# Each step of four attentions in two halves between the blocks of the weight groups

## The chip, the cores and the metric

One Trainium2 chip, of which the kernel uses one core. The core has a tensor engine (PE; its weight loads are listed apart as PEld), a vector engine (DVE), a scalar engine (ACT), GpSimd (POOL) and SyncE (SP), which issues the transfers. Each engine works through its own instructions strictly in order, and they wait for each other by semaphores. The metric is the device time of one execution in microseconds.

## The reference

Two transformer blocks in float32 on one sequence of 512 tokens and 1024 features.

```python
def first_block(x, ...):
    h = rms_norm(x, norm1_g)
    qa, ka, va, hy_in, qc, kc, vc, gate_logits = split(h @ w_in)
    out_a = window_attention(rope(norm(qa)), rope(norm(ka)), va, sink_a)      # 8 heads, |t - s| <= 128
    out_b = hyena_branch(hy_in, ...)
    out_c = rms_norm(diff_attention(rope(norm(qc)), rope(norm(kc)), vc, lam)) # 4 heads, softmax1 - lam * softmax2
    merged = g[0] * (out_a @ w_oa) + g[1] * (out_b @ w_ob) + g[2] * (out_c @ w_oc)
    x = x + merged @ w_out
    return x + (silu(h2 @ w1) * (h2 @ w3)) @ w2                               # h2 = rms_norm(x, norm2_g)

def second_block(x, ...):
    fq, fk, fv, f_logit, sq, sk, sv = split(rmsnorm(x) @ w_in_2)
    o_fox = fox_attention(fq, fk, fv, log_sigmoid(f_logit + bias))            # 8 heads, causal, softmax with decay
    # stick breaking, 8 heads: z = q.k / 8, s < t
    # A[t, s] = sigmoid(z[t, s]) * prod over s < j < t of (1 - sigmoid(z[t, j]));  o_sb = A @ v
    x = x + concat(rmsnorm(o_fox), rmsnorm(o_sb)) @ w_out_2
    u = causal_dwconv(rmsnorm(x) @ w_up)
    return rmsnorm(x + (silu(gate) * val) @ w_down)
```

## The kernel before, in words

**Weights and blocks.** All projections are streamed: 240 slots of 128 x 1024 numbers come from HBM, and each is split into a high and a low part of a reduced type, `whi` on ACT (L1357) and `wlo` on DVE (L785; on POOL, L1797, for `qc`, `kc`, `vc` and the hyena groups), so that three matmuls give the accuracy of one in float32. A group of weights (`qc`, `kc`, `gA0`, `sv`, `fq`, ...) is 4 or 2 slots, and a slot is worked off in four blocks, each of 6 matmuls over 512 columns into banks `ps0` to `ps3` of the accumulator memory. After the last slot of a group each block's bank is evacuated by ACT or DVE.

**Work beside.** The four attentions have no stretch of their own, apart from the end of the last one. Each is a Python generator, one copy for each engine, put in `flow.beside`. After each block `slots` calls `flow.pump` for some steps of it: `group(..., rate)` says how many steps go into the four blocks of a slot, so rate 2 puts one step after every second block, rate 4 one after every block. What a step has on an engine stands in that engine's queue at that place. `window` (36 steps, rate 2) runs beside `qc`, `kc`, `vc`, `gA0`, `gA1`; `differential` (22 steps, rate 2) beside `bA0`, `bA1`, `gC0`, `gC1`; `stick` (37 steps) beside `sv` (rate 1), `fq` (2), `fk` and `fv` (4); `fox` (38 steps) starts in `fv` with three steps, and the rest follows with no blocks between ("the drain"). Rotary work of `qc` and `kc` (DVE L952 to L970, partly POOL) stands in `flow.later` between the slots.

**A step.** Unit u is one head of one block of 128 query tokens. PE has three kinds of work in step u: `turn`, the transposes (L353) of an earlier unit's weights; `scores` of unit u (or u and u + 1 at every other step) into `ps4`/`ps5`; `values` of a unit still earlier. In the window attention DVE's `lowest(u)` reads the scores and takes a row extreme (L1003), ACT's `shares(u)` takes the exponential (L1491, L1493), DVE's `shares(u-1)` divides (L1009 to L1013), and ACT copies the transposed tile `PT` (L1500). In the differential attention DVE has `highest(u)` (two of L1057, L1059) and `combine(u-1)` (L1066 to L1072, which makes `Pc`); after the fourth head of a block of queries its output goes through squares (DVE L1087), a root and a scale on POOL (L1919 to L1925, which write `ocs`), four transposes of `ocs` into `ps6` in PE's step (L353), and `ochi`/`oclo` (ACT L1546, DVE L1091).

**The stick-breaking step.** For unit u, with n the width of its scores (units 0 to 7 have 512 columns, 8 to 15 have 128, 16 to 23 have 384, 24 to 31 have 256): ACT `copy(u)` brings the scores from `ps4`/`ps5` to `zb` (L1646); DVE `parts(u)` makes |z| and min(-z, 0) from it (L1191, L1192); ACT `logs(u)` (L1651, L1653); DVE `sums(u)`, a scan (L1199); POOL adds, `sum(u)` (L1964); ACT `weights(u)` (L1658); PE `turn(u)`; DVE `evac(u)` to `PT` (L1207); PE `values(u)`. In step u DVE has `sums(u-2)`, `evac(u-4)`, `parts(u)` in this order, and POOL `sum(u-2)`. ACT has `copy(u)`, `logs(u-1)`, `weights(u-2)`. The copy waits for the scores alone, and for POOL's sum three units back, which frees its `zb`.

**Fox step.** In the drain PE has `scores(u)`, `turn(u-3)`, `values(u-5)`, DVE `lowest(u)` and the evacuation of even units, ACT `shares(u)` and that of odd units.

Of the kernel before, what the change touches and what calls it, by code (L numbers as in the profile page):

```python
# [129 lines left out]
def build(nc, d, out):  # L130
# [208 lines left out]
    def tensor_program(t):  # L339
# [165 lines left out]
        def window():  # L505
# [107 lines left out]
        def stick():  # L613
# [49 lines left out]
        def fox():  # L663
# [68 lines left out]
        rotary_group("qc", 2, 4, 2)  # L732
        rotary_group("kc", 3, 4, 2)
        group("vc", hT, h_ready(0), lambda b: (vc_c, b + 1), 2)
        flow.flush()
        for half in range(2):
            group("gA%d" % half, hT, h_ready(0), lambda b: (g_t, 8 + 4 * half + b + 1), 2)
        flow.drain()
        flow.beside.append(differential())
        for half in range(2):  # L740
            group("bA%d" % half, lambda k: (oahi[:, k, :], oalo[:, k, :]), lambda k, b: w.wait_ge(oa_lo, 4),
                  lambda b: (b_v, 8 + 4 * half + b + 1), 2)
        for half in range(2):
            group("gC%d" % half, hT, h_ready(0), lambda b: (g_t, 16 + 4 * half + b + 1), 2)
# [15 lines left out]
        group("sv", hT, h_ready(2), lambda b: (sv_c, b + 1))  # L760
        flow.beside.append(fox())
        group("fq", hT, h_ready(2), lambda b: (h_v, 2 * (b // 2) + 2) if b % 2 else (h_a, 2 * (b // 2) + 2), 2)
        group("fk", hT, h_ready(2), lambda b: (h_v, 4 + 2 * (b // 2) + 2) if b % 2 else (h_a, 4 + 2 * (b // 2) + 2), 4)
        group("fv", hT, h_ready(2), lambda b: (fv_c, b + 1), 4)
# [10 lines left out]
    def vector_program(v):  # L775
# [215 lines left out]
        def window():  # L991
# [57 lines left out]
        def differential():  # L1049
# [129 lines left out]
        def stick():  # L1179
# [42 lines left out]
        def fox():  # L1222
# [33 lines left out]
            for u in range(38):  # L1256
                while u == 3 and not fox_go:
                    yield
                if u < 32:
                    lowest(u)  # L1260
                if 3 <= u < 35 and (u - 3) % 2 == 0:
                    evac(u - 3)
# [39 lines left out]
        group("qc", rotary(2, 8), 2)  # L1302
        group("kc", rotary(3, 8), 2)
        group("vc", none, 2)
        flow.flush()
        for half in range(2):
            group("gA%d" % half, none, 2)
        flow.drain()
        flow.beside.append(differential())
        for half in range(2):  # L1310
            group("bA%d" % half, branch(1, half), 2)
        for half in range(2):
            group("gC%d" % half, none, 2)
# [12 lines left out]
        group("sv", none)  # L1326
        flow.beside.append(fox())
        group("fq", heads_out(Qf), 2)
        group("fk", heads_out(Kf), 4)
        group("fv", none, 4)  # L1330
# [15 lines left out]
    def scalar_program(a):  # L1346
# [138 lines left out]
        def window():  # L1485
# [21 lines left out]
            for u in range(36):  # L1507
                if 3 <= u < 35:
                    evac(u - 3)
                if u < 32:  # L1510
# [10 lines left out]
        def differential():  # L1521
# [27 lines left out]
            for u in range(22):  # L1549
                if 2 <= u < 18:  # L1550
                    evac(u - 2)
                if u < 16:
# [87 lines left out]
        def stick():  # L1640
# [19 lines left out]
            for u in range(37):  # L1660
                if u < 32:
                    copy(u)
                if 1 <= u <= 32:
                    logs(u - 1)
                if 2 <= u < 34:
                    weights(u - 2)
                if u in (15, 23, 31):
# [14 lines left out]
        def fox():  # L1682
# [14 lines left out]
            for u in range(38):  # L1697
                while u == 3 and not fox_go:
                    yield
                if u < 32:  # L1700
                    shares(u)
                if 3 <= u < 35 and (u - 3) % 2:
                    evac(u - 3)
# [46 lines left out]
        group("qc", rotary(2, 8, qcT), 2)  # L1750
        group("kc", rotary(3, 8, kcT), 2)
        group("vc", values, 2)
        flow.flush()
        for half in range(2):
            group("gA%d" % half, gates(1, half), 2)
        flow.drain()
        flow.beside.append(differential())
        for half in range(2):
            group("bA%d" % half, none, 2)
        for half in range(2):  # L1760
            group("gC%d" % half, gates(2, half), 2)
# [484 lines left out]
```

## Time and profile before

| | |
|---|---|
| median of 3 runs | 1731.5 us (1728.58 to 1731.97) |
| the profiled execution | 1728.6 us, of which its span is 1726.8 us |
| PE busy | 1648.0 us (95%), granted clock 0.989 of full on average |
| DVE, ACT, POOL busy | 833.2, 658.0, 271.0 us |

| stretch | us | PE idle in it, us |
|---|---|---|
| window, 311 to 480 | 169 | 4.9 |
| differential, 487 to 598 | 111 | 8.2 |
| stick beside `sv` and `fq`, 1105 to 1170 | 65 | 4.1 |
| stick beside `fq` end, `fk`, `fv`, 1170 to 1250 | 80 | 9.6 |
| fox, the drain, 1250 to 1306 | 56 | 0.8 |

The times in the rows below count from the start of the span. A row of the order in time gives its start, its duration, the engine, the line, what it writes and reads (without the numbers of the buffers), how many instructions it stands for, and in square brackets how long the engine had been idle and what ended that.

### The profile page before, as it was taken

How to read it: one execution, taken by the hardware profiler on the slowest of the kernel's cores; microseconds unless marked ns; L12 is line 12 of the kernel's file. 1: busy time of each engine (PE TensorE's matmuls, PEld its weight loads, DVE VectorE, ACT ScalarE, POOL GpSimd, SP SyncE). 2: the span in 40 equal slices, each digit the busy share in tenths (PEclk: the TensorE clock that was granted, in tenths of full speed). 3: DMA queues.
4: the chain of work that ended last, by engine and by line, in shares of the span. 5: the costliest groups of instructions: out<-in, count | busy, mean ns of one | idle time of the engine just before them, and what ended most of it. 6: DMA issues, size and time to landing. Idle time of an engine off the chain costs nothing.

```text
span 1726.8 us, 19076 instructions
## 1 busy us (share of the span) xinstructions
PE 1648.0 (95%) x7552; PEld 1301.6 (75%) x7552; DVE 833.2 (48%) x1332; ACT 658.0 (38%) x1150; POOL 271.0 (16%) x280
## 2 busy tenths in 40 slices
PE   5999998999999999999999998898999999999997
PEld 3566787767766787888888886676678788888886
DVE  5446455366356464333332224376663465556323
ACT  4332223454444433333222223366563344444221
POOL 3443205462012111000000002023200100000001
PEclk9999999999999999999999999999999999999999
DMA  6111112211121332333332321221102233233332
GB/s 227 56 67 47 49 49 85 80 50 62 61 62 49 110 98 73 98 98 98 98 98 98 97 87 63 93 69 42 50 13 74 74 97 98 95 94 92 111 98 72
DMA packets 39221, 139.51 MB, mean 81 GB/s; under 512 B 4331, under 2 KB 4971, under 8 KB 38940
## 3 DMA queue, kind: packets, MB, share of 16 engines
q1 hardware_dynamic: 39132, 138.29, 25.0%
q8 instruction: 60, 0.98, 0.2%
q14 instruction: 29, 0.24, 0.0%
HBM read 136.14 MB, written 2.10 MB: 80 GB/s over the span
## 4 chain that ended last, share of the span: by engine, by line
PE 84%; DVE 7%; POOL 4%; ACT 3%; issue 2%; DMA 1%; SPq 0%; DVEq 0%; POOLq 0%; ACTq 0%
PE ps L350 80%; PE ps L353 3%; DVE raw L970 1%; ACT whi L1357 1%; POOL small L1817 1%; POOL st L1881 1%; POOL small L1811 0%; DVE wlo L785 0%; ACT junk L1369 0%; DMA x<-in_x 0%; POOL small L1814 0%; DVE st L1057 0%; DVE xs L796 0%; DVE W L1199 0%; DVE olo L1162 0%
## 5 line engine op out<-in xcount | busy, mean ns | idle before, releaser
L785 DVE TENSOR_TENSOR wlo<-wraw,whi 128x1024 fp32r<-128x1024 f32 (+2 forms) x220 | 267.0, 1214 | 527.3 <-ACT whi L1357 527.1
L350 PE MATMUL ps<-hThi,whi 128*128 128x512 f32 x1128 | 453.6, 402 | 2.2 <-DVE hTlo L801 1.4
L1357 ACT ACTIVATE whi<-wraw 128x1024 fp32r<-128x1024 f32 (+2 forms) x244 | 253.0, 1038 | 511.6 <-PE ps L350 506.0
L350 PE MATMUL ps<-hThi,wlo 128*128 128x512 f32 x1128 | 441.0, 391 | 0.0
L350 PE MATMUL ps<-hTlo,whi 128*128 128x512 f32 x1128 | 440.9, 391 | 0.0
L350 PEld LDWEIGHTS ps<-hThi,whi 128*128 128x128 f32 x1128 | 212.7, 189 | 57.4 <-issue 15.7
L350 PEld LDWEIGHTS ps<-hThi,wlo 128*128 128x128 f32 x1128 | 212.6, 189 | 45.4
L350 PEld LDWEIGHTS ps<-hTlo,whi 128*128 128x128 f32 x1128 | 212.8, 189 | 44.5 <-issue 2.9
L350 PE MATMUL ps<-whi,achi 128*128 128x512 f32 x352 | 136.9, 389 | 0.0
L350 PE MATMUL ps<-wlo,achi 128*128 128x512 f32 x352 | 136.9, 389 | 0.0
L350 PE MATMUL ps<-whi,aclo 128*128 128x512 f32 x352 | 136.9, 389 | 0.0
L350 PE MATMUL ps<-whi,hThi 128*128 128x512 f32 (+1 forms) x288 | 115.2, 400 | 0.0
L1811 POOL TENSOR_SCALAR small<-small 128x1 f32<-128x1 f32 x20 | 10.0, 499 | 649.7 <-ACT junk L1369 648.5
L350 PE MATMUL ps<-wlo,hThi 128*128 128x512 f32 (+1 forms) x288 | 110.6, 384 | 0.0
L350 PE MATMUL ps<-whi,hTlo 128*128 128x512 f32 (+1 forms) x288 | 110.5, 384 | 0.0
L350 PEld LDWEIGHTS ps<-wlo,achi 128*128 128x128 f32 x352 | 66.1, 188 | 13.8
L350 PEld LDWEIGHTS ps<-whi,achi 128*128 128x128 f32 x352 | 66.1, 188 | 13.7
L350 PEld LDWEIGHTS ps<-whi,aclo 128*128 128x128 f32 x352 | 66.1, 188 | 13.7
L1797 POOL TENSOR_TENSOR wlo<-wraw,whi 128x1024 fp32r<-128x1024 f32 x24 | 58.8, 2453 | 82.4 <-ACT whi L1357 82.4
L350 PEld LDWEIGHTS ps<-whi,hThi 128*128 128x128 f32 x288 | 55.6, 193 | 13.6 <-issue 4.4
L350 PEld LDWEIGHTS ps<-whi,hTlo 128*128 128x128 f32 x288 | 55.4, 192 | 10.7
L350 PEld LDWEIGHTS ps<-wlo,hThi 128*128 128x128 f32 x288 | 55.6, 193 | 9.5 <-issue 0.5
(272 smaller groups left out, 2151.0 us busy)
## 6 DMA issues: line engine op xcount, KB each, us to landing
wraw<-in_ws SPq DMA_DIRECT2D x236, 512.0 KB, 3.5
x<-in_x SPq DMA_DIRECT2D x4, 512.0 KB, 7.8
x<-in_x SPq DMA_DIRECT2D x1, 2048.0 KB, 8.4
out<-xs SPq DMA_DIRECT2D x8, 256.0 KB, 2.0
dec<-in_dec SPq DMA_DIRECT2D x1, 1024.0 KB, 15.9
wraw<-in_ws SPq DMA_DIRECT2D x4, 256.0 KB, 2.6
vec<-in_vec SPq DMA_DIRECT2D x1, 788.0 KB, 4.9
w<-in_w SPq DMA_DIRECT2D x1, 512.0 KB, 14.3
```

The lines of the kernel that those rows point to most:

```text
L350: return t.matmul(o, l, r, start=first, stop=last)
L353: return t.transpose(ps[b][:, c * 128:(c + 1) * 128], src, ident)
L785: v.tensor_tensor(wlo[h][:, 0:width(i)], wraw[h][:, 0:width(i)], whi[h][:, 0:width(i)].bitcast(F32), ALU.subtract).then_inc(lo_done[h], 1)
L970: v.tensor_tensor(r_, q0, q1, ALU.add).then_inc(r_a, 1)
L1357: a.activation(whi[h][:, 0:width(i)], wraw[h][:, 0:width(i)], ACT.Copy).then_inc(hi_done[h], 1)
L1797: g.tensor_tensor(wlo[h][:, 0:width(i)], wraw[h][:, 0:width(i)], whi[h][:, 0:width(i)].bitcast(F32), ALU.subtract).then_inc(lo_done[h], 1)
L1811: g.tensor_scalar(small[:, i:i + 1], small[:, c:c + 1], 1.0 / D, EPS, ALU.mult, ALU.add).then_inc(n_rs, 1)
L1817: g.tensor_tensor(small[:, 8 + i:9 + i], small[:, 4 + i:5 + i], col("mhalf"), ALU.pow).then_inc(n_rs, 1)
L1881: g.tensor_tensor(ss, ms, col("mhalf", 0, n_heads), ALU.pow).then_inc(r_r, 1)
```

## The change

The generators of all four attentions yield twice in each step, and the rates are doubled, so that a step covers the same blocks as before. Where a step has two blocks (`window`, `differential`, and `stick` beside `fq`) its first half stands after the first of them and its second half after the second, which was the place of the whole step; `stick` beside `sv` has a step in four blocks, its halves after the second and the fourth. Where a step has one block (`stick` beside `fk` and `fv`) or none (the drain of `fox`) the two halves follow each other directly. The first half holds `turn` on PE, and on the others what belongs to earlier units; the second holds `scores` and `values`, and what belongs to unit u. For that the order inside a step changes at these places: DVE's `shares(u-1)` and `combine(u-1)` now stand ahead of `lowest(u)` and `highest(u)`, ACT's `logs(u-1)` and `weights(u-2)` ahead of `copy(u)`, and in `fox` the transposes and evacuations ahead of `scores`, `lowest` and `shares`. No instruction is added or taken away on any engine.

```diff
@@ PE: window, differential, stick
             for u in range(36):
                 if 3 <= u < 35:
                     turn(u - 3)
+                yield
                 if u < 32 and u % 2 == 0:
                     scores(u)
                     scores(u + 1)
...
             for u in range(22):
                 if 2 <= u < 18:
                     turn(u - 2)
+                yield
                 if u < 16:
                     scores(u)
...
             for u in range(37):
                 if 4 <= u < 36:
                     turn(u - 4)
+                yield
                 if u < 32 and u % 2 == 0:
                     scores(u)
@@ PE: fox
+                if 3 <= u < 35:
+                    turn(u - 3)
+                yield
                 if u < 32:
                     scores(u)
-                if 3 <= u < 35:
-                    turn(u - 3)
@@ the rates, the same on every engine
-        rotary_group("qc", 2, 4, 2)
+        rotary_group("qc", 2, 4, 4)
...
-        group("sv", hT, h_ready(2), lambda b: (sv_c, b + 1))
+        group("sv", hT, h_ready(2), lambda b: (sv_c, b + 1), rate=2)
...
-        group("fv", hT, h_ready(2), lambda b: (fv_c, b + 1), 4)
+        group("fv", hT, h_ready(2), lambda b: (fv_c, b + 1), 8)
@@ DVE: window
             for u in range(36):
+                if 1 <= u <= 32:
+                    shares(u - 1)
+                yield
                 if u < 32:
                     lowest(u)
-                if 1 <= u <= 32:
-                    shares(u - 1)
@@ DVE: differential
             for u in range(22):
+                if 1 <= u <= 16:
+                    combine(u - 1)
+                yield
                 if u < 16:
                     highest(u)
-                if 1 <= u <= 16:
-                    combine(u - 1)
@@ DVE: stick
                 if 4 <= u < 36:
                     evac(u - 4)
+                yield
                 if u < 32:
                     parts(u)
@@ ACT: stick
             for u in range(37):
-                if u < 32:
-                    copy(u)
                 if 1 <= u <= 32:
                     logs(u - 1)
                 if 2 <= u < 34:
                     weights(u - 2)
+                yield
+                if u < 32:
+                    copy(u)
```

ACT beside `fk`, before: two steps of the stick-breaking attention, from the copy of one unit's scores on (`zb` are the copied scores, `Lb` the logarithms and weights of units one and two back).

```order
L1646 ACTIVATE zb0_188<-ps4 128x384
L1651 ACTIVATE Lb2_185<-Lb2_185 128x384
L1653 ACTIVATE Lb2_185<-Lb2_185,vec_60 128x384
L1658 ACTIVATE Lb1_184<-Lb1_184 128x384
L1646 ACTIVATE zb1_189<-ps5 128x384
L1651 ACTIVATE Lb3_186<-Lb3_186 128x384
L1653 ACTIVATE Lb3_186<-Lb3_186,vec_60 128x384
```

The same instructions now (the lines are ten further down):

```order
L1661 ACTIVATE Lb2_185<-Lb2_185 128x384
L1663 ACTIVATE Lb2_185<-Lb2_185,vec_60 128x384
L1668 ACTIVATE Lb1_184<-Lb1_184 128x384
L1656 ACTIVATE zb0_188<-ps4 128x384
L1661 ACTIVATE Lb3_186<-Lb3_186 128x384
L1663 ACTIVATE Lb3_186<-Lb3_186,vec_60 128x384
L1668 ACTIVATE Lb2_185<-Lb2_185 128x384
```

The copy of unit u moved from ahead of the logarithms to behind the weights of unit u - 2.

DVE in the differential attention, before: the unit that ends the second block of queries (its two row extremes), the combination of the unit before it, the squares of that block's output, and then the split of a weight slot.

```order
L1057 TENSOR_REDUCE st_129<-ps5 128x1
L1059 TENSOR_SCALAR st_129<-st_129 128x1
L1066 RECIPROCAL st_129<-st_129 128x1
L1068 SCALAR_TENSOR_TENSOR st_129<-st_129,small_61 128x1
L1070 RECIPROCAL st_129<-st_129 128x1
L1072 SCALAR_TENSOR_TENSOR Pc0_136<-Pc1_137,st_129,Pc0_136 128x512
L1087 TENSOR_REDUCE st_129<-oc_142 128x4
L785 TENSOR_TENSOR wlo1_58<-wraw1_52,whi1_55 128x1024
```

The same place now:

```order
L1039 SCALAR_TENSOR_TENSOR gate1_108<-gate1_108,ps2 128x512
L1071 RECIPROCAL st_129<-st_129 128x1
L1073 SCALAR_TENSOR_TENSOR st_129<-st_129,small_61 128x1
L1075 RECIPROCAL st_129<-st_129 128x1
L1077 SCALAR_TENSOR_TENSOR Pc0_136<-Pc1_137,st_129,Pc0_136 128x512
L1039 SCALAR_TENSOR_TENSOR gate1_108<-gate1_108,ps3 128x512
L1062 TENSOR_REDUCE st_129<-ps4 128x1
L1064 TENSOR_SCALAR st_129<-st_129 128x1
L1062 TENSOR_REDUCE st_129<-ps5 128x1
L1064 TENSOR_SCALAR st_129<-st_129 128x1
L1092 TENSOR_REDUCE st_129<-oc_142 128x4
L789 TENSOR_TENSOR wlo1_58<-wraw1_52,whi1_55 128x1024
```

The combination moved ahead of the extremes, and ahead of the evacuation of the second of two blocks; the squares follow the extremes directly.

PE in the window attention, beside `qc`, at the first transposes of a unit:

```order
 L350 MATMUL ps2<-whi0_54,hTlo_50 128x512
+L353 MATMUL ps6<-vec_60,T8_0_121 128x128 x2
 L350 MATMUL ps3<-whi0_54,hThi_49 128x512
 L350 MATMUL ps3<-wlo0_57,hThi_49 128x512
...
 L350 MATMUL ps3<-wlo0_57,hThi_49 128x512
 L350 MATMUL ps3<-whi0_54,hTlo_50 128x512
-L353 MATMUL ps6<-vec_60,T8_0_121 128x128 x2
```

The transposes moved ahead of one block; scores and values stand where they stood.

## Rows read from the trace of the kernel before

**Rows 1.** Table by stretch: start:end, us, busy of PE, PEld, DVE, ACT, POOL, clock, DMA, GB/s.

```profile
1170.00:1250.00 80.00, 70.45 (x385) 52.81 (x383) 54.86 (x112) 50.09 (x120) 23.84 (x34) 0.98 0.14 47
```

**Rows 2.** PE's waits by what it waited for: us in total, times, longest us.

```profile
PE ps L353 <- POOL ocs L1925: 7.0, 3, 3.0
...
PE ps L353 <- DVE PT L1207: 4.8, 7, 1.7
```

**Rows 3.** Order in time on PE, window attention, around two transposes of a unit.

```profile
325.88 0.38 PE L353 MATMUL ps<-vec,T 128*128 128x128 f32 x2
326.01 0.48 PE L350 MATMUL ps<-whi,hThi 128*128 128x512 f32 x1
...
328.85 0.38 PE L353 MATMUL ps<-vec,T 128*128 128x128 f32 x2
329.16 0.70 PE L350 MATMUL ps<-kaT,qaT 64*128 64x256 f32 x4
```

**Rows 4.** Order in time, window attention, rotary work on DVE just before 356.45.

```profile
356.45 0.60 DVE L1003 CUSTOM_DVE_ANT_0 T<-ps,maskA,small 128x384 f32<-128x384 f32 x1
...
357.10 0.61 ACT L1491 ACTIVATE T<-T,st 128x384 f32<-128x384 f32 x1 [5.62 <-DVE st L1003]
...
357.12 0.91 PE L350 MATMUL ps<-kaT,qaT 64*128 64x384 f32 x2 [1.48 <-DVE st L1003]
...
357.93 0.60 DVE L1003 CUSTOM_DVE_ANT_0 T<-ps,maskA,small 128x384 f32<-128x384 f32 x1
```

**Rows 5.** Order in time, differential attention: the first wait, and the outputs' way.

```profile
501.64 0.66 PE L353 MATMUL ps<-vec,Pc 128*128 128x128 f32 x4 [1.27 <-DVE Pc L1072]
...
533.51 0.75 DVE L1091 SCALAR_TENSOR_TENSOR oclo<-ps,vec,ochi 128x512 fp32r<-128x512 f32 x1 [0.52 <-ACT ochi L1546]
...
548.63 0.69 DVE L1057 TENSOR_REDUCE st<-ps 128x1 f32<-128x512 f32 x1 [1.89 <-PE ps L350]
...
550.21 0.16 DVE L1066 RECIPROCAL st<-st 128x1 f32<-128x1 f32 x1
...
551.40 0.68 DVE L1087 TENSOR_REDUCE st<-oc 128x4 f32<-128x512 f32 x1
...
554.82 1.04 POOL L1925 TENSOR_TENSOR ocs<-ocs,st 128x512 f32<-128x512 f32 x1
...
555.91 0.66 PE L353 MATMUL ps<-vec,ocs 128*128 128x128 f32 x4 [1.96 <-POOL ocs L1925]
```

**Rows 6.** Order in time, stick-breaking attention, two units of 384 columns.

```profile
1203.86 0.49 ACT L1646 ACTIVATE zb<-ps 128x384 f32<-128x384 f32 x1 [2.79 <-PE ps L350]
...
1204.38 0.56 DVE L1191 SCALAR_TENSOR_TENSOR Lb<-zb 128x384 f32<-128x384 f32 x1 [1.18 <-ACT zb L1646]
...
1205.52 0.96 DVE L1199 TENSOR_TENSOR_SCAN W<-W,Lb 128x384 f32<-128x384 f32 x1 [0.31 <-ACT Lb L1653]
...
1206.55 1.00 POOL L1964 TENSOR_TENSOR Lb<-zb,W 128x384 f32<-128x384 f32 x1 [3.37 <-DVE W L1199]
...
1206.88 1.09 DVE L1191 SCALAR_TENSOR_TENSOR Lb<-zb 128x384 f32<-128x384 f32 x1
...
1207.58 0.53 ACT L1658 ACTIVATE Lb<-Lb 128x384 f32<-128x384 f32 x1 [0.32 <-POOL Lb L1964]
...
1210.21 1.22 DVE L785 TENSOR_TENSOR wlo<-wraw,whi 128x1024 fp32r<-128x1024 f32 x1
```

**Rows 7.** The same attention: the copies of units 17 and 31, and between them.

```profile
1185.13 0.47 ACT L1646 ACTIVATE zb<-ps 128x384 f32<-128x384 f32 x1
...
1214.11 0.68 DVE L1278 COPY Kf<-ps 64x512 f32<-64x512 f32 x1 [0.23 <-PE ps L350]
...
1218.62 0.73 POOL L1964 TENSOR_TENSOR Lb<-zb,W 128x256 f32<-128x256 f32 x1 [1.16 <-DVE W L1199]
...
1233.33 0.36 ACT L1646 ACTIVATE zb<-ps 128x256 f32<-128x256 f32 x1
```

**Rows 8.** The table by stretch, 3.5 us in the stick-breaking attention after a wait of PE.

```profile
1199.00:1202.50 3.50, 3.50 (x13) 2.54 (x12) 2.49 (x4) 2.04 (x6) 3.16 (x5) 0.56 0.00 0
```

More of the change, by code:

```diff
@@ L731, in tensor_program @@
         flow.beside.append(window())
-        rotary_group("qc", 2, 4, 2)
-        rotary_group("kc", 3, 4, 2)
-        group("vc", hT, h_ready(0), lambda b: (vc_c, b + 1), 2)
+        rotary_group("qc", 2, 4, 4)
+        rotary_group("kc", 3, 4, 4)
+        group("vc", hT, h_ready(0), lambda b: (vc_c, b + 1), 4)
         flow.flush()
         for half in range(2):
-            group("gA%d" % half, hT, h_ready(0), lambda b: (g_t, 8 + 4 * half + b + 1), 2)
+            group("gA%d" % half, hT, h_ready(0), lambda b: (g_t, 8 + 4 * half + b + 1), 4)
         flow.drain()
@@ L741, in tensor_program @@
             group("bA%d" % half, lambda k: (oahi[:, k, :], oalo[:, k, :]), lambda k, b: w.wait_ge(oa_lo, 4),
-                  lambda b: (b_v, 8 + 4 * half + b + 1), 2)
+                  lambda b: (b_v, 8 + 4 * half + b + 1), 4)
         for half in range(2):
-            group("gC%d" % half, hT, h_ready(0), lambda b: (g_t, 16 + 4 * half + b + 1), 2)
+            group("gC%d" % half, hT, h_ready(0), lambda b: (g_t, 16 + 4 * half + b + 1), 4)
         flow.drain()
@@ L1258, in fox @@
                     yield
+                if 3 <= u < 35 and (u - 3) % 2 == 0:
+                    evac(u - 3)
+                yield
                 if u < 32:
                     lowest(u)
-                if 3 <= u < 35 and (u - 3) % 2 == 0:
-                    evac(u - 3)
                 if u == 8:
@@ L1301, in vector_program @@
         flow.beside.append(window())
-        group("qc", rotary(2, 8), 2)
-        group("kc", rotary(3, 8), 2)
-        group("vc", none, 2)
+        group("qc", rotary(2, 8), 4)
+        group("kc", rotary(3, 8), 4)
+        group("vc", none, 4)
         flow.flush()
         for half in range(2):
-            group("gA%d" % half, none, 2)
+            group("gA%d" % half, none, 4)
         flow.drain()
@@ L1310, in vector_program @@
         for half in range(2):
-            group("bA%d" % half, branch(1, half), 2)
+            group("bA%d" % half, branch(1, half), 4)
         for half in range(2):
-            group("gC%d" % half, none, 2)
+            group("gC%d" % half, none, 4)
         flow.drain()
@@ L1699, in fox @@
                     yield
+                if 3 <= u < 35 and (u - 3) % 2:
+                    evac(u - 3)
+                yield
                 if u < 32:
                     shares(u)
-                if 3 <= u < 35 and (u - 3) % 2:
-                    evac(u - 3)
                 if u == 7:
@@ L1749, in scalar_program @@
         flow.beside.append(window())
-        group("qc", rotary(2, 8, qcT), 2)
-        group("kc", rotary(3, 8, kcT), 2)
-        group("vc", values, 2)
+        group("qc", rotary(2, 8, qcT), 4)
+        group("kc", rotary(3, 8, kcT), 4)
+        group("vc", values, 4)
         flow.flush()
         for half in range(2):
-            group("gA%d" % half, gates(1, half), 2)
+            group("gA%d" % half, gates(1, half), 4)
         flow.drain()
@@ L1758, in scalar_program @@
         for half in range(2):
-            group("bA%d" % half, none, 2)
+            group("bA%d" % half, none, 4)
         for half in range(2):
-            group("gC%d" % half, gates(2, half), 2)
+            group("gC%d" % half, gates(2, half), 4)
         flow.drain()
@@ L1774, in scalar_program @@
         flow.beside.append(stick())
-        group("sv", copied(sv, sv_c))
+        group("sv", copied(sv, sv_c), rate=2)
         flow.beside.append(fox())
-        group("fq", heads_out(Qf), 2)
-        group("fk", heads_out(Kf), 4)
-        group("fv", copied(fv, fv_c), 4)
+        group("fq", heads_out(Qf), 4)
+        group("fk", heads_out(Kf), 8)
+        group("fv", copied(fv, fv_c), 8)
         fox_go.append(True)
@@ L2001, in gpsimd_program @@
             group("bB%d" % half, none, 2)
-        flow.beside.append(iter(range(36)))
-        group("qc", rotary(2, 8), 2)
-        group("kc", rotary(3, 8), 2)
-        group("vc", none, 2)
+        flow.beside.append(iter(range(72)))
+        group("qc", rotary(2, 8), 4)
+        group("kc", rotary(3, 8), 4)
+        group("vc", none, 4)
         flow.flush()
         for half in range(2):
-            group("gA%d" % half, none, 2)
+            group("gA%d" % half, none, 4)
         flow.drain()
@@ L2011, in gpsimd_program @@
         for half in range(2):
-            group("bA%d" % half, branch(1, half), 2)
+            group("bA%d" % half, branch(1, half), 4)
         for half in range(2):
-            group("gC%d" % half, none, 2)
+            group("gC%d" % half, none, 4)
         flow.drain()
@@ L2026, in gpsimd_program @@
         flow.beside.append(stick())
-        group("sv", none)
+        group("sv", none, rate=2)
         flow.beside.append(fox())
-        group("fq", none, 2)
-        group("fk", none, 4)
-        group("fv", none, 4)
+        group("fq", none, 4)
+        group("fk", none, 8)
+        group("fv", none, 8)
         fox_go.append(True)
```

18 lines of the change are left out of this document (12 added, 6 removed).

## The prediction, made before the kernel ran

> **What bounds the kernel now.** I read the table of times first, then the table by stretch, then PE's list of waits, and last the order in time at the places that this list names. PE is busy for 1648.0 of 1726.8 us, so work that the others do costs nothing unless PE waits for it, and the four attentions are to be judged by PE's idle time: 4.9, 8.2, 4.1, 9.6 and 0.8 us in the five stretches of the second table. The largest is the stick-breaking attention beside the end of `fq`, `fk` and `fv`, with PE busy for 70.45 of 80 us and no other engine over 54.86 [rows 1]: there PE waits for a chain of engines and not for a full one. The list of waits gives 7.0 us to POOL's `ocs`, in the differential attention, and 4.8 us to the evacuation `PT` in the stick-breaking one [rows 2].
>
> **The change on PE.** The instructions are the same; what is new is that a block stands between transposes and scores. In the window attention two transposes cost 0.13 us if a block follows and 0.31 us if scores follow [rows 3]. But the block that was one run of 12 matmuls becomes two of 6, and starting again costs something: the block at 326.01 begins with 0.48 us in place of 0.39. From these I take 0.14 us for the restart and 0.09 us for scores that follow a block (the same 0.09), so 0.13 + 0.14 + 0.09 - 0.31 = +0.05 us in a step with scores, and nothing in one with values alone; a mean of 0.03 us. That is 32 steps x 0.03 = +1.0 in the window attention, 16 x 0.03 = +0.5 in the differential one and 8 x 0.03 = +0.2 in the stick-breaking one beside `fq`. Beside `fk` and `fv` and in the drain no block stands between the halves, so PE's order in the former is as it was. The bounds are 0 and 3 us in all.
>
> **Window attention.** Elsewhere than at the rotary work DVE has time to spare and its new order costs nothing. At the rotary work it is behind, and there it now does `shares(u-1)` ahead of `lowest(u)`. [Rows 4] show one such place: `lowest` at 356.45 lets PE's scores start at 357.12, after a wait of 1.48 us; `lowest` of the next unit comes at 357.93, so the shares between them take 1.48 - 0.60 = 0.88 us. In the new order these 0.88 us stand ahead of the first `lowest`, and PE waits so much longer; and the next shares have to wait for ACT's exponential (0.61 us and two short ones, about 1.2 us), which the old order covered with the next `lowest`. I count two such places at 0.88 us less a little that transposes win by earlier shares: **+1.5 us**, bounds -1 and +6 (five places at 1.2 us).
>
> **Differential attention.** The first wait, 1.27 us for `Pc` at 501.64 [rows 5], should go, since `combine` no longer stands behind `highest`: -1.3. For the output of a block of queries the way is `highest`, `combine`, squares, four instructions on POOL, transposes. At 550.21 to 551.40 `combine` takes 1.19 us of it, PE waits 1.96 us at the end of it, and DVE has been idle for 1.89 us before `highest` [rows 5], so here the combination finds room and PE's wait shrinks by up to 1.19. What is late next is `ps6`: it is free only after `oclo`, which waits for ACT's `ochi` (row at 533.51), which stands behind an exponential of the unit then under way; the following unit's transposes now come one block sooner. I allow 0.3 us for that: -0.9. For the first output DVE has no such idle time (in its order two gate evacuations stand there back to back, and the combination moves between them): -0.2. The third has the list's longest wait of 3.0 [rows 2] and room: -1.1. Sum -1.3 - 0.9 - 0.2 - 1.1 = **-3.5 us**, bounds -5 and -0.5.
>
> **Stick-breaking attention.** Before, ACT copied unit u's scores as soon as they were there. Now `copy(u)` stands behind `weights(u-2)`. These wait for POOL's `sum(u-2)`, which waits for DVE's `sums(u-2)`, which stands in DVE's queue right behind `parts(u-1)`, which wait for `copy(u-1)`. So there is a closed loop of one step, where before two steps shared one. Its length for 384 columns from [rows 6]: copy to `parts` 1204.38 - 1203.86 = 0.52; `parts` to scan 1205.52 - 1204.38 less the 0.31 that the scan waited for ACT = 0.83; scan to POOL 1.03; POOL to weights 1.03; weights to the next copy 0.43 (0.53 less the 0.1 by which such rows overlap). Sum 3.84 us. For 256 columns POOL's row is 0.73 against 1.00 [rows 7]; at about that ratio the loop is 2.8 us. From the copy of unit 17 to that of unit 31 are 7 steps of 384 columns, one between and 6 of 256: 7 x 3.84 + 3.3 + 6 x 2.8 = 47.0. Into DVE's place between `parts` and `sums` fall further the splits of three slots (1.22 each, [rows 6]) and two pairs of `Kf` copies (2 x 0.68 each, [rows 7]): 47.0 + 3.7 + 2.7 = 53.4 us. The trace of before has 1233.33 - 1185.13 = 48.2 us [rows 7]. That is +5.2 us. After it PE had little slack, so I let it through: **+5.2 us**. Bounds: 0, if `wlo` and `Kf` find DVE idle and PE's waits of before are the same waits; +10, if output tiles and `whi` on ACT fall in the loop too. With 512 columns, beside `sv`, the loop is about 4.7 us by the same scaling and a step has a slot's time there: nothing. With 128 columns it is shorter than a step's blocks: nothing.
>
> **Drain of fox.** PE is idle for 0.8 of 56 us. The new order puts transposes ahead of scores; the transposes' input is three units old and ready: 0, bounds -0.3 and +1.
>
> **Sum.** +1.7 (PE) + 1.5 - 3.5 + 5.2 = +4.9 us. On the profiled execution, 1728.6 us, that gives 1733.5; this execution is 2.9 us below the median of the three, 1731.5, so against the median it is **1736.4**, which I round to 1736.5.
>
> **The rivals.** *The loop is hidden.* If three quarters of the loop's interruptions fall into DVE's idle time and PE's slack takes the rest, stick costs 0 to 1 us, and the sum is +1.7 + 1.5 - 3.5 + 0.5 = +0.2: 1731.7. For it speaks that before, too, the splits stood in the chain and PE kept 3.4 us a step; against it, that 3.84 us is more than 3.4 without any interruption. *Faster.* DVE's `parts` take 0.56 us at 1204.38 and 1.09 us at 1206.88, beside a POOL instruction that began at 1206.55 [rows 6]. In the new order `parts(u)` come after POOL's sum by their place in the loop and are never beside it. If this is what made `PT` late, the 4.8 us of [rows 2] go, the loop costs nothing, and with both attentions of the first block as above: +1.7 + 1.5 - 3.5 - 4.8 = -5.1: 1726.4. The Trainium skill, "Advanced Engine Details and Errata", section "GPSIMD Details", says that GpSimd shares a read and a write interface with the vector engine and conflicts with its instructions that have two SBUF inputs. `parts` begin with such an instruction, so by that rule the trace agrees, and this rival is the time that it gives. Against it: shorter `parts` shorten the loop, but I have already counted them at 0.56. *Worse.* From five rotary places at 1.2 us, +6 in place of +1.5, and PE waiting longer at each step of the stick-breaking loop, so that its clock falls: in 3.5 us after a wait it was at 0.56 [rows 8], which is 1.5 us of work lost each time. It decides if PE's waits in the loop pass what they were at 1196. With three falls: +4.9 + 4.5 + 4.5 = +13.9: 1745.4. *It doesn't do what it says*: beside `fk` and `fv` no block stands between the halves, by the order of the instructions; that is part of the forecast, since all it does there is the new order on ACT.
>
> **How the numbers follow.** Forecast (loop costs 3 to 8 us) 0.50; hidden 0.22; faster 0.15; worse 0.13. The predicted time is the forecast's, 1736.5. A measurement of this kernel can tell about 0.2%, 3.5 us, from no change. Of the forecast's 0.50 some 0.43 lies above 1735.0 and 0.07 below; of the hidden case 0.20 within and 0.02 faster. So slower 0.43 + 0.13 = 0.56, same 0.07 + 0.20 = 0.27, faster 0.15 + 0.02 = 0.17. The range leaves out the lower part of the faster case and the upper half of the worse one: 1728 to 1747.
>
> **What would show it.** In the changed kernel's trace, copies L1656 of units 17 to 31 spread over 53 us in place of 48.2, each copy behind a weights instruction that waited for POOL L1964 (right), or at the old pace (wrong, hidden). PE's waits for `ocs` sum to about 5 in place of 7.0, the one for `Pc` is gone. At rotary work PE waits about 1 us longer for L1003. If the stretch beside `fk` and `fv` is not longer than its 80 us, the forecast is wrong, whatever the total.

## The result: 13.8 us slower, a forecast on the right side and at a third of the size

| | before | changed |
|---|---|---|
| median, us | 1730.0 (4 runs, 1726.4 to 1732.0) | 1743.8 (4 runs, 1741.4 to 1746.2) |
| ratio | | 1.0083, 95% interval 1.0067 to 1.0098 |
| profiled span, us; mean clock | 1726.8; 0.989 | 1739.6; 0.987 |

The forecast was +4.9 us on the median known then, 1736.5, with a range to 1747. The measured time lies in the range, but the difference, +13.8 us, is almost 9 us more than forecast; the upper end of the range was set by the rival "worse".

The two kernels have the same 5784 matmuls of weight blocks in the same order, so the start of the k-th of them can be set against the same one of the kernel before. This table, worked out from the two traces, is the account to which everything below refers. (Its positions count from each trace's own zero, the rows from the start of the span; for the changed kernel that differs by 0.2 us, which falls out of every cost. A difference that exists before the first attention is start-up: -2.2 us at 248 us.)

| from, in the time of before | changed minus before at its end, us | cost of the stretch | forecast |
|---|---|---|---|
| window, 302 to 486 | -2.2 to +1.0 | +3.1 | +2.5 |
| differential, 486 to 589 | +1.0 to +5.1 | +4.1 | -3.0 |
| stick beside `sv` and `fq`, 1103 to 1175 | +5.8 to +7.3 | +1.5 | +0.2 |
| stick beside `fk` and `fv`, 1175 to 1238 | +7.3 to +14.7 | +7.5 | +5.2 |
| the drain of fox, 1238 to 1302 | +14.7 to +13.0 | -1.7 | 0 |

The attentions cost 14.5 us together; start-up (-2.2), +0.6 between the first block's attentions and the second's and -0.7 behind the drain lie outside them and make it 12.3 at the last block. So the largest surprise is not in the stick-breaking attention but in the differential one, where a gain was forecast.

The table by stretch of the changed kernel (stretch, us, busy time of PE, PEld, DVE, ACT, POOL, granted clock, share of the DMA engines, GB/s), for the differential attention and for the stick-breaking one beside `fk` and `fv`; the latter answers to [rows 1]:

```profile
487.00:603.00 116.00, 107.70 (x534) 76.52 (x533) 76.56 (x159) 50.19 (x103) 22.43 (x24) 0.99 0.15 50
...
1177.00:1264.00 87.00, 74.54 (x389) 55.22 (x389) 52.51 (x113) 51.59 (x119) 22.59 (x34) 0.96 0.14 41
```

PE's idle time is 8.3 us in the first (8.2 before) and 12.5 in the second (9.6 before), so in the differential attention the loss doesn't show as idle time: PE's own rows got longer, by a wait inside a row (four scores that take 1.13 us elsewhere have 1.91 at 503.74) and by a lower clock (it was at half for 3.4 us from 536 on, and in the kernel before nowhere in this attention). DVE is busy for 6.4 us more in the differential attention (76.56 against 70.12) for the same instructions. PE's waits in the changed kernel, to be read against [rows 2]:

```profile
PE ps L353 <- DVE PT L1213: 9.1, 10, 1.8
...
PE ps L353 <- POOL ocs L1937: 4.5, 3, 2.3
...
PE ps L350 <- DVE st L1007: 4.1, 3, 2.2
...
PE ps L353 <- DVE st L1071: 2.0, 2, 1.8
...
PE ps L353 <- DVE st L1007: 1.6, 1, 1.6
PE ps L353 <- DVE Pc L1077: 1.5, 1, 1.5
```

L1007 is the window attention's row extreme, for which PE had waited less in the kernel before:

```profile
PE ps L353 <- DVE st L1003: 2.5, 2, 1.4
PE ps L350 <- DVE st L1003: 2.3, 2, 1.5
```

The waits for `ocs` did shrink by 2.5 us, as the forecast had it. The wait for `Pc` did not go, and one for L1071 is new: L1071 is the instruction that follows `oclo` on DVE, so what PE waits for there is the bank `ps6`.

### The profile page after: what moved, and what is told of

Read it like the earlier page. It is cut to its first block, busy times and chain, and to the rows that moved or that the text cites. A ratio compares the mean times of both kernels' runs of the same rounds, so it can differ in the third digit from the quotient of the medians.

```text
span 1739.6 us, 19077 instructions
## 1 busy us (share of the span) xinstructions
PE 1656.4 (95%) x7552; PEld 1299.9 (75%) x7552; DVE 830.0 (48%) x1332; ACT 660.3 (38%) x1150; POOL 270.6 (16%) x280
## 4 chain that ended last, share of the span: by engine, by line
PE 79%; DVE 9%; ACT 4%; POOL 4%; issue 3%; DMA 1%; SPq 0%; DVEq 0%; POOLq 0%; ACTq 0%
PE ps L350 76%; PE ps L353 3%; DVE W L1205 1%; POOL Lb L1977 1%; ACT whi L1365 1%; DVE wlo L789 1%; POOL small L1823 1%; POOL small L1829 1%; ACT Pc L1538 1%; ACT zb L1656 1%; DVE st L1062 0%; DVE st L1073 0%; ACT Lb L1668 0%; DVE st L1013 0%; POOL small L1826 0%
## 5 line engine op out<-in xcount | busy, mean ns | idle before, releaser
L350 PEld LDWEIGHTS ps<-whi,achi 128*128 128x128 f32 x352 | 66.1, 188 | 13.8
```

The costliest lines, as they stand in the source:

```text
L350: return t.matmul(o, l, r, start=first, stop=last)
```

## The stick-breaking attention: the loop

Order in time in the changed kernel, two units of 384 columns, to be read against [rows 6]:

```profile
1214.99 0.47 ACT L1656 ACTIVATE zb<-ps 128x384 f32<-128x384 f32 x1
...
1215.50 0.56 DVE L1197 SCALAR_TENSOR_TENSOR Lb<-zb 128x384 f32<-128x384 f32 x1 [1.62 <-ACT zb L1656]
...
1216.25 0.95 DVE L1205 TENSOR_TENSOR_SCAN W<-W,Lb 128x384 f32<-128x384 f32 x1
...
1217.28 1.00 POOL L1977 TENSOR_TENSOR Lb<-zb,W 128x384 f32<-128x384 f32 x1 [2.75 <-DVE W L1205]
...
1217.79 0.63 PE L353 MATMUL ps<-vec,W 128*128 128x128 f32 x4 [1.82 <-DVE PT L1213]
...
1218.31 0.52 ACT L1668 ACTIVATE Lb<-Lb 128x384 f32<-128x384 f32 x1 [1.04 <-POOL Lb L1977]
1218.74 0.47 ACT L1656 ACTIVATE zb<-ps 128x384 f32<-128x384 f32 x1
```

Copy, `parts`, scan, POOL, weights, next copy: 1218.74 - 1214.99 = 3.75 us, where the prediction had 3.84. Each engine waits for the one before it. DVE waited 45.5 us in all for `zb` before `parts`, 30 of 32 times (12.9 us and 12 times before), the sign of a closed loop. Copy to copy from unit 17 to unit 31 took 1250.02 - 1194.49 = 55.5 us.

**The order on ACT set back.** First half empty, the second half as before:

```diff
             for u in range(37):
+                yield
+                if u < 32:
+                    copy(u)
                 if 1 <= u <= 32:
                     logs(u - 1)
                 if 2 <= u < 34:
                     weights(u - 2)
-                yield
-                if u < 32:
-                    copy(u)
```

> The changed kernel with ACT's order in the stick-breaking step alone set back: all of it in the second half, copy, logs, weights. Loop theory (the copy behind the weights closes a loop of one step, 3.75 us at 384 columns, 4.70 at 512): PE gets back the 7.5 us that it lost beside fk and fv and 1.5 of those beside sv and fq: 1743.8 - 9 = 1735. Rival (the halves on PE and DVE, or the clock after PE's waits, cost it): not more than 2 us come back, 1742 to 1744.

1734.9 us. By the positions of the blocks the stick-breaking attention cost 0.0 us (8.22 late at 1103 and at 1238), against 9.0 in the changed kernel, and the copies of units 17 to 31 spread over 48.3 us (before 48.2). By one trace and by the medians (8.9 us apart) all of the nine microseconds are ACT's order; the halves on PE, DVE and POOL cost nothing here.

**The order on ACT alone**, in the kernel before, without halves or new rates: logs, weights, copy.

> The kernel before, no halves and no new rates, with one thing of the change: ACT's order in the stick-breaking step is logs, weights, copy. Loop theory: it alone costs what the stick-breaking stage cost in the changed kernel, +9 (7.5 of it beside fk and fv): 1729 + 9 = 1738. Rival (it needs the halves, which put the copy a block later beside fq): less than 4, under 1733.

1740.3 us, ratio 1.0067 (1.0048 to 1.0086): +11.6 us. The loop does not need the halves; they even soften it a little beside `sv` and `fq` (3.7 us here, 1.5 in the changed kernel). Beside `fk` and `fv` the cost is 9.9 us and the copies spread over 57.9 us. PE's clock was down twice in this stretch, for about 10 and 7 us; in the changed kernel it was twice, for 3.4 us each, and before once for 3.4. Part of the difference between 7.5 and 9.9 us may be that.

**Copy in the middle**: logs, copy, weights, the rest as in the changed kernel.

```diff
                 if 1 <= u <= 32:
                     logs(u - 1)
-                if 2 <= u < 34:
-                    weights(u - 2)
                 yield
                 if u < 32:
                     copy(u)
+                if 2 <= u < 34:
+                    weights(u - 2)
```

> The changed kernel with one ACT instruction of the stick-breaking step moved: the copy between the logarithms and the weights (logs, copy, weights). Loop theory: what closes the loop is the copy behind the weights, which wait for POOL; behind the logarithms alone it waits only for DVE's parts of the unit before, a loop of about 2.2 us (0.5 + 0.5 + 1.2), which PE never sees. So the time is that of e4, 1735. Rival (any work of an earlier unit ahead of the copy costs its time, ACT being short of it): the logarithms are 1.1 us a step, and a good half of the 9 us stays: 1740.

1735.0 us, as with the old order, although 1.1 us of ACT's work still stand ahead of the copy. It is not work ahead of the copy that costs, but the one instruction among it that waits for POOL. In this trace the stick-breaking attention was even 2.8 us shorter than before, of which more below.

## The differential attention: three things that the forecast lacked or priced too low

**The attention alone** in the kernel before:

> The kernel before with the change in the differential attention alone (halves, rates, combine ahead of highest). In the trace of the changed kernel PE fell 4.1 us further behind in this attention (0.97 us late at its start, 5.10 at its end). If that is the attention's own doing, this kernel takes 1730.0 + 4 = 1734 us, and PE's positions after it are about 4 us later than in the kernel before. If it was the late start (a different meeting of evacuations and weight splits) that did it, it takes my forecast of -3: 1727.

1732.8 us, +3.3 (ratio 1.0011, interval 1.0000 to 1.0023). The ratio isn't the quotient of the medians, here and below; its interval reaches 1, so the whole time barely shows the loss, and the reading rests on the positions. They give the cost of the stretch as 4.13 us, as in the changed kernel (4.1) and in the two with its code there and another order on ACT (4.1 each): it is its own doing. For the same instructions as before, DVE took longer. Order in time in the changed kernel, where the first wait was to go:

```profile
498.57 0.68 DVE L1039 SCALAR_TENSOR_TENSOR gate<-gate,ps 128x512 f32<-128x512 f32 x1
...
499.33 1.28 POOL L1925 TENSOR_TENSOR merged<-merged,gate 128x512 f32<-128x512 f32 x1 [96.04 <-DVE gate L1039]
499.36 1.27 DVE L1073 SCALAR_TENSOR_TENSOR st<-st,small 128x1 f32<-128x1 f32 x1
...
500.74 0.75 DVE L1077 SCALAR_TENSOR_TENSOR Pc<-Pc,st,Pc 128x512 f32<-128x512 f32 x1
501.40 0.68 DVE L1039 SCALAR_TENSOR_TENSOR gate<-gate,ps 128x512 f32<-128x512 f32 x1
```

L1073 works on one element in each partition. Its usual time is 0.22 us; here it begins 0.03 us after a POOL instruction of 1.28 us and ends with it. Seven of its 16 were so (0.94 to 1.27 us, 6.4 us over in all, which is DVE's surplus above). `combine` used to stand behind two evacuations of gates; now it stands directly behind one, and an evacuation is what starts POOL's addition. The Trainium skill, "Advanced Engine Details and Errata", section "GPSIMD Details", says that GpSimd shares a read and a write interface with the vector engine and conflicts with its instructions that have two SBUF inputs. The trace agrees, and adds that an instruction on one element waits until the POOL instruction has ended.

**One input in place of two**, in `combine` and in the window attention's `shares`:

```diff
-                v.scalar_tensor_tensor(st[:, o + 4:o + 5], st[:, o + 3:o + 4], lam, st[:, o + 2:o + 3], ALU.mult, ALU.mult)
+                v.tensor_scalar(st[:, o + 4:o + 5], st[:, o + 3:o + 4], lam, st[:, o + 2:o + 3], ALU.mult, ALU.mult)
...
-                v.tensor_tensor(st[:, c + 4:c + 5], st[:, c + 2:c + 3], st[:, c + 3:c + 4], ALU.add)
+                v.tensor_scalar(st[:, c + 4:c + 5], st[:, c + 2:c + 3], st[:, c + 3:c + 4], None, ALU.add)
```

> The changed kernel with two short DVE instructions of one element per partition written with one tensor input and a scalar pointer in place of two tensor inputs, the same arithmetic: the product in combine (L1073) and the sum in the window attention's shares (L1013). Theory 1, they wait for a whole POOL instruction because of their second input: the seven slow ones of L1073 (0.94 to 1.27 us in place of 0.22, 6.4 us over) and the slow ones of L1013 (up to 2.16 us in place of 0.15) fall to 0.22 and 0.15, and the time falls by 3 to 5 us: 1743.8 - 4 = 1740, the differential stretch by 3. Theory 2, they are slow for another reason (DVE's queue, the semaphore's way): the slow ones stay, and so does the time, 1743.8.

1737.7 us, 6.1 below the changed kernel. The positions give the window attention +1.0 in place of +3.1 and the differential one +2.4 in place of +4.1, so 3.8 us by the trace (the other 2.3 us between the medians I can't place), and no L1073 or L1013 is slow any more. PE's waits for the window's row extreme, 5.7 us in the changed kernel, are 3.6. First the window's sum, in the changed kernel, beside POOL's split of a weight slot:

```profile
348.04 2.39 POOL L1809 TENSOR_TENSOR wlo<-wraw,whi 128x1024 fp32r<-128x1024 f32 x1
...
348.28 2.16 DVE L1013 TENSOR_TENSOR st<-st 128x1 f32<-128x1 f32 x1 [0.96 <-ACT st L1501]
```

and with one input:

```profile
349.55 2.38 POOL L1809 TENSOR_TENSOR wlo<-wraw,whi 128x1024 fp32r<-128x1024 f32 x1
...
349.80 0.21 DVE L1013 TENSOR_SCALAR st<-st 128x1 f32<-128x1 f32 x1 [0.96 <-ACT st L1501]
```

0.21 us beside the same POOL instruction: the second input is what waits. In the differential attention the gain is smaller, since the next two-input instruction takes over part of the wait. With one input, the place shown above:

```profile
498.70 1.28 POOL L1925 TENSOR_TENSOR merged<-merged,gate 128x512 f32<-128x512 f32 x1 [95.59 <-DVE gate L1039]
498.73 0.27 DVE L1073 TENSOR_SCALAR st<-st,small 128x1 f32<-128x1 f32 x1
...
499.11 1.42 DVE L1077 SCALAR_TENSOR_TENSOR Pc<-Pc,st,Pc 128x512 f32<-128x512 f32 x1
```

L1077 takes 1.42 us in place of 0.75. So `combine` ends 0.3 us sooner than in the changed kernel and not 1.05 us.

**The bank.** What is left is PE's side. In the changed kernel, behind the second block of queries, to be read against [rows 5]:

```profile
562.15 0.69 ACT L1538 ACTIVATE Pc<-ps,st 128x512 f32<-128x512 f32 x1 [3.65 <-DVE st L1064]
...
562.93 0.69 ACT L1538 ACTIVATE Pc<-ps,st 128x512 f32<-128x512 f32 x1
...
563.61 0.68 ACT L1555 ACTIVATE ochi<-ps,vec 128x512 fp32r<-128x512 f32 x1
...
564.32 0.75 DVE L1096 SCALAR_TENSOR_TENSOR oclo<-ps,vec,ochi 128x512 fp32r<-128x512 f32 x1 [1.43 <-ACT ochi L1555]
...
565.22 0.63 PE L353 MATMUL ps<-vec,Pc 128*128 128x128 f32 x4 [1.79 <-DVE st L1071]
```

The chain is the one that the prediction named (exponentials, `ochi`, `oclo`, `ps6`), for which it allowed 0.3 us. It took 1.79 us here. By the block positions 1.73 us were won at `ocs` and 2.33 lost at the next transposes. And it came a second time, behind the first block of queries, for which the forecast had no `ps6` term at all. In the changed kernel that wait is only 0.2 us, with the clock down there; in the kernel with this attention alone both are whole (L1067 is there what L1071 is here), and the positions give 2.3 us lost at each:

```profile
PE ps L353 <- DVE st L1067: 3.6, 2, 1.8
```

Twice 2.3 us is more than the whole 4.1, so this is the largest of the three; against it stand the gains at `ocs`.

**The two halves of the cause apart.** Only PE's transposes one block early, DVE and ACT in their old order in the second half:

> The kernel before with the other thing: PE's transposes of the differential attention one block early, DVE and ACT in their old order in the second half. Theory: the first wait is for the same Pc but has lost a block of cover, +1.4; the transposes behind ocs wait for ps6, +0.9 twice (from 533.4 to 534.3 in the trace of before); the split blocks +0.3: +3.5, 1733. Rival (combine first is what makes ps6 late): +0.3 to +1.7 only, 1730 to 1731.

1736.8 us, +8.0 (ratio 1.0046, 1.0029 to 1.0064). Both theories missed it. PE's waits in this attention:

```profile
PE ps L353 <- DVE Pc L1073: 7.7, 13, 1.4
PE ps L353 <- POOL ocs L1928: 4.9, 3, 2.3
```

By the positions 8.7 us went in this attention. The bank is not in the list; PE waits in nearly every step for `combine`, 0.46 us where all is regular and 1.35 at two places. A block between transposes and scores is a block less between `combine` and the transposes. So in the change the early transposes need `combine` early, and the early `combine` meets POOL.

And only `combine` in a first half (with one input), PE's order as before:

> The kernel before with one thing of the change in the differential attention: DVE's combine stands in a first half, a block ahead of highest; PE's order is the one of before, and ACT's evacuation stays with the transposes; the product in combine has one tensor input, as in e3. Theory (PE's transposes one block early are what lost the cover; combine first is good by itself): the wait for Pc (1.27) goes, those for ocs shrink by 0.2, 1.2 and 1.1, no wait for ps6 comes: -1.3 - 2.5 = -3.8, 1729.5 - 3.8 = 1725.7. Rival (combine first delays highest and so ACT's exponentials, ochi and oclo, and ps6 is late by that): the wait for ps6 of 1.5 twice comes here too, 1729.

1730.3 us, ratio 1.0010 (0.9998 to 1.0021): no gain. The wait for `Pc` went and those for `ocs` fell to 4.5, as expected, and no wait for the bank came, against the rival. But in place of the wait for `Pc` stands one of the scores:

```profile
501.18 2.69 PE L350 MATMUL ps<-kcT,qcT 64*128 64x512 f32 x4 [1.54 <-ACT Pc L1531]
```

`highest` now stands behind `combine` and the second gate, so the exponential that frees the scores' banks comes later. So the wait for the bank `ps6` comes neither from the early transposes alone nor from the early `combine` alone, but from both together. And the clock fell. The same stretch in this kernel (first line), and in the next kernel below, which has the same code there (second line):

```profile
501.00:509.00 8.00, 7.82 (x20) 5.14 (x21) 5.80 (x14) 3.89 (x10) 2.54 (x2) 0.57 0.00 1
```

```profile
499.00:507.00 8.00, 7.41 (x34) 4.69 (x35) 5.80 (x13) 4.79 (x11) 2.84 (x3) 1.00 0.00 1
```

After the same wait of 1.54 us PE ran at half its clock (1.2 GHz in place of 2.4) for 6.8 us in one and not in the other: 20 matmuls in place of 34. The attention cost 4.1 us in one and 0.7 in the other.

## The window attention alone

> The kernel before with the halves in the window attention alone. In the changed kernel's trace this attention cost 3.1 us, 2.1 of which went with the one-input forms of e3. If the costs of the attentions add, 1729 + 3.1 = 1732; the sum over the four is then 3.1 + 4.1 + 9.0 - 1.7 = 14.5, beside 13.8 measured.

1735.3 us, ratio 1.0032 (1.0017 to 1.0047). By the positions of the blocks the attention cost 2.3 us to 486 us; another 1.5 us came at about 581 us, where nothing is changed and the clock of this execution was down for 3 us. The medians give more, 6.6 us, and I can't say from one profile what the rest is. The cost per attention is known to about the price of one or two such falls, no better: the same window code cost 2.3 us here, 3.1 in the changed kernel and 5.8 in the one with the copy in the middle, and in the kernel with early transposes, which leaves the window as it was, 1.6 us were lost there beside a fall of 6.8 us.

## What was won: the drain of fox

The kernel before with the new order of the fox steps alone:

```diff
+                if 3 <= u < 35:
+                    turn(u - 3)
                 if u < 32:
                     scores(u)
-                if 3 <= u < 35:
-                    turn(u - 3)
```

> The kernel before with the new order of the fox steps alone (transposes ahead of scores on PE, evacuations ahead of lowest on DVE and of shares on ACT), with no halves anywhere. In the changed kernel's trace PE won back 1.7 us in the drain. If the order does that by itself, 1730.0 - 1.7 = 1728.3. If it was only lateness of the stick-breaking attention absorbed at the seam, no change: 1730.

1727.3 us, ratio 0.9983 (0.9969 to 0.9998). The positions give -1.74 us in the drain, as in the changed kernel (-1.73). It is the steadiest figure here: all eight kernels with this order have -1.7, the five others 0.0. PE in this kernel:

```profile
1270.15 1.02 PE L350 MATMUL ps<-Kf,Qf 66*128 66x512 f32 x2
1271.01 0.33 PE L350 MATMUL ps<-fv,PTf 128*128 128x64 f32 x2
1271.18 0.61 PE L353 MATMUL ps<-vec,Tf 128*128 128x128 f32 x4
1271.62 0.39 PE L350 MATMUL ps<-Kf,Qf 66*128 66x128 f32 x2
1271.85 1.00 PE L350 MATMUL ps<-fv,PTf 128*128 128x64 f32 x8
1272.69 0.28 PE L353 MATMUL ps<-vec,Tf 128*128 128x128 f32 x1
1272.80 0.81 PE L350 MATMUL ps<-Kf,Qf 66*128 66x384 f32 x2
```

and in the kernel before, the same kinds in the old order:

```profile
1271.10 0.44 PE L350 MATMUL ps<-Kf,Qf 66*128 66x128 f32 x2
1271.37 0.60 PE L353 MATMUL ps<-vec,Tf 128*128 128x128 f32 x4
1271.81 1.00 PE L350 MATMUL ps<-fv,PTf 128*128 128x64 f32 x8
1272.65 1.08 PE L350 MATMUL ps<-Kf,Qf 66*128 66x512 f32 x2
1273.57 0.27 PE L353 MATMUL ps<-vec,Tf 128*128 128x128 f32 x1
1273.68 0.33 PE L350 MATMUL ps<-fv,PTf 128*128 128x64 f32 x2
1273.85 0.44 PE L350 MATMUL ps<-Kf,Qf 66*128 66x128 f32 x2
```

There is no wait in either. Two steps take 2.75 us before (1273.85 - 1271.10) and 2.65 now (1272.80 - 1270.15). The scores of 512 columns run to the next instruction in 0.86 us between transposes and values and in 0.92 between values and transposes, those of 128 columns in 0.23 against 0.27: 0.05 us a step, 32 times. What an instruction costs on PE depends on its neighbours; whether on the one before or the one behind it isn't shown, since both changed.

## Together

The kernel before with the fox order and with combine first:

> What seemed to help, put together: the kernel before with the fox order of e2 and combine first of e5. If both gains stand and add: 1729.5 - 1.7 - 3.8 = 1724. If combine first brings nothing: 1727.5 as in e2.

1731.4 us, ratio 1.0016 (1.0005 to 1.0026): it doesn't add. By the positions the drain won its 1.7 us and the differential attention cost 0.7, with the clock down at 531 us. Another 3.2 us went between 600 and 1103 us, where nothing is changed: the clock was at half there for 20 us in place of 10 in the kernel before. Whether the early `combine` has to do with that isn't shown.

With the fox order and the halves in the stick-breaking attention, the copy in the middle:

> The kernel before with the halves in the stick-breaking attention alone, its copy between logarithms and weights as in e7, and with the fox order. In e7's trace the stick-breaking stage was 2.8 us shorter than in all others, because a wait of PE that had been followed by 3.5 us at half clock was shorter there. If that comes with the order, 1729 - 2.8 - 1.7 = 1724.5; if the clock's fall was spared by chance, 1727.3 as in e2.

1725.3 us, ratio 0.9981 (0.9970 to 0.9993). It is the fastest by its median, 3.4 us under the kernel before, but by its ratio no faster than the fox order alone (0.9983). Its trace has the stick-breaking stretch 2.5 us shorter, copies of units 17 to 31 in 46.5 us in place of 48.2, and no fall of the clock where [rows 8] show one:

```profile
1195.00:1203.00 8.00, 5.97 (x36) 4.48 (x36) 6.73 (x11) 5.07 (x11) 4.65 (x6) 1.00 0.21 69
```

Without halves, the copy in the middle and the fox order:

> As e10, without halves: the steps of the stick-breaking attention are whole, and ACT's order in them is logs, copy, weights. If the order on ACT is what spared the wait, as e10; if the halves are, as e2, 1727.3.

1727.9 us, ratio 0.9992 (0.9978 to 1.0006). Here the clock fell at 1196 us again; the copies spread over 47.4 us, the stretch was 0.9 us shorter than before. The two kernels with halves and the copy in the middle were spared the fall, and all the others had it. But the wait before it is no shorter with halves: PE waits 0.97 us for `PT` at that place in all three kernels with the copy in the middle, with and without halves, where the kernel before waits 1.67. So it is the order on ACT that shortens the wait. Why the clock fell in this kernel and not in the two others stays open; at half clock for 3.4 us it is worth about the 1.6 us between them.

## Why the prediction was right or wrong, point by point

- **The sum** was +4.9 us and the positions give +14.5 for the same five stretches. Of the 9.6 us between them the differential attention has 7.1, the stick-breaking one 3.6 and the window 0.6, and the drain takes 1.7 back. That the time lies within the range is luck in good part.
- **The loop on ACT** was right in place, mechanism and length (3.84 forecast, 3.75 measured for 384 columns); setting the order back returned all of it and the order alone in the kernel before brought it. Its term was too small, 5.2 against 7.5 us beside `fk` and `fv`: 53.4 us forecast for units 17 to 31, 55.5 measured, and PE's clock was down for one stretch of some 3 us more than before, about 1.5 us. The sentence "with 512 columns a step has a slot's time there: nothing" was wrong: the loop is 4.70 us (from `parts` at 1146.10 to 1150.79) and 5.85 with a slot's split in it, and the stretch cost 1.5 us.
- **The split blocks on PE**, +0.03 us a step, were right in kind and about twice too dear: in regular steps of the differential attention a block comes 0.36 us later and the next one 0.35 sooner, so +0.01 to +0.02.
- **The window attention**, +2.5 forecast and +3.1 measured, was right in sum by luck and in part wrong in mechanism. PE's waits for the row extreme rose by 0.9 us (from 4.8 to 5.7), near the 1 us forecast. I had counted `shares` ahead of `lowest` and ACT's exponential uncovered; 2.1 of the 3.1 us went when the short sum in `shares` had one input. The exponential was uncovered (rows [0.96 <-ACT st L1501] above), but that was not what made it dear.
- **The differential attention**, -3.5 and +0.5 forecast and +4.1 measured, is the step that failed. "The first wait should go, since combine no longer stands behind highest": it did not, since the transposes too came a block sooner, and since `combine` met POOL (1.27 us in place of 0.22). "I allow 0.3 us for that", for `ps6`: 1.79 us of waiting at the second output, and as much again at the first, for which nothing was allowed. I had the chain and priced it from positions of before, in which `highest` still came first. The waits for `ocs` fell by 2.5 us, as the sum had it (2.2).
- **The drain**, forecast as nothing since PE had no wait there: -1.7. PE without waits is not PE whose order doesn't matter.
- **The rival "faster"** used the shared interface in the wrong place. I had seen a two-input instruction slow beside POOL in the stick-breaking attention, where the change takes the meeting away, and did not look where the change makes new ones. Its premise held: all 32 of these instructions now take their short time (15.7 us in all in place of 23.2), but DVE was not what the attention waited for any more, the loop was. New meetings came behind gate evacuations and beside POOL's splits.
- **The rival "worse"** (1745.4) came nearest to the time, by a sum of falls of the clock and rotary places that is only in part what happened: the mean clock fell from 0.989 to 0.987, which is two falls of 3.4 us more, and the loop and `ps6` are in none of its terms beyond the forecast's.

## What to carry to other kernels

When work is moved on an in-order engine, draw for each moved instruction the circle of waits through all engines back to itself: an instruction that waits for no one (the copy), put behind one that waits for the end of a long chain, closed a loop of a whole step and cost 9 us without adding any work. Before two engines that share an interface are set side by side, look at what starts the one (here the evacuation of a gate starts POOL's addition) and which two-input instructions of the other come right behind it, however short they are. And a step split around a block takes that block's cover from whatever stands behind it.

## What the runs showed of the hardware

- A DVE instruction with two SBUF inputs and a single element in each partition takes up to 2.16 us beside a POOL instruction of 2.39 us, and 0.21 us with one input and a scalar pointer beside the same one; its successor with two inputs then takes the rest of the wait (1.42 in place of 0.75 us).
- The granted clock fell to half after waits of PE of 1.5 to 2.3 us in some executions and not in others of the same code (8 us at 0.57 against 1.00 after the same wait of 1.54 us). Such falls go with the spread of 1724 to 1735 us of the kernel before (its run of 1723.95 us has a mean clock of 0.992, that of 1733.9 us 0.983), and they bound what one profile can tell of a stretch.
- Scores between transposes and values cost PE 0.05 us less than between values and transposes, 1.7 us over the drain, with no wait in the rows shown.
